# Two out-projections with operands split into high and low parts, for token tiles 2 to 4

## The chip, the cores and the metric

The kernel runs on one core of a Trainium2 chip. The time is device time in microseconds (us) of one execution. TensorE (PE) multiplies, VectorE (DVE), ScalarE (ACT) and GpSimd (POOL) work element by element, and SyncE (SP) issues most DMAs. All of them run their own instruction stream in order and wait for each other through semaphores.

## The reference

576 tokens (512 of a prompt, 64 of eight samples) of width 1024 go through two layers. Layer 0 mixes tokens by a gated delta rule and causal pooling, layer 1 by a linear recurrence with learned gates. Both end in an out-projection, and a mixture of 16 experts follows:

```python
y = jnp.concatenate([o_a, o_b], axis=-1) @ w_out          # layer 0
...
y = (hs * y_br) @ w_out                                   # layer 1
...
x = layer_norm(ALPHA * x + h, ln_mix_g[layer], ln_mix_b[layer])
f = moe(x, router_w, router_bias, moe_w_gate[layer], moe_w_up[layer], moe_w_down[layer])
x = layer_norm(ALPHA * x + f, ln_ffn_g[layer], ln_ffn_b[layer])
```

## The kernel before

Tokens lie in five tiles, four of 128 rows and one of 64. The mixer's result lies transposed in `XT` (eight blocks of 128 channels by 576 tokens). The out-projection multiplies a tile's columns of `XT` (stationary) with the eight weight blocks (`WO_A` in layer 0, `WO_B` in layer 1; 128 x 1024 each, taken in halves of 512 columns) and sums over the eight blocks in two PSUM banks. These matmuls are in plain fp32. The projections and the experts don't do that: they split each operand into a high part rounded to fp32r and a low rest, and sum three fp32r matmuls (high x high, high x low, low x high). ACT makes high parts by a copy, DVE makes low parts by a subtraction.

`out_and_route` is PE's order around it. In layer 0, `out_part` (line 967) does tiles 0 and 1, partly early, between steps of the sample states. In layer 1, line 1017 does tiles 0 and 1 block by block, as the recurrence delivers blocks (`mix_a`). In front of the last of the eight blocks stands a small transpose (line 1013) whose result DVE copies out (line 2382). Then `out_projection` (line 980) does tiles 2 and 3, the transposes of the normed tiles 0 and 1 follow (line 611), then tile 4, the transposes of tiles 2 and 3, the router's logits (line 991), the transposes and logits of tile 4. Banks alternate by tile, so that tile t waits for DVE to have read tile t-2 (`norm_sum`).

`norm` is the layer norm after the mixer (q = 0 and 2). For each tile DVE adds the bank to `X` and takes statistics (lines 2029 to 2038), ACT takes the root and scales, DVE applies gain and bias (lines 2052, 2054). After tile 4, ACT rounds and DVE splits the first expert's gate weights, and only then both copy out the last transposed tile.

The recurrence of layer 1 (`mixer1` of DVE) works in two groups of four channel blocks. A block takes a product, a few small operations, a scan over 576 tokens and a last product that writes `XT` and counts `mix_a` (line 2366). Most of these operations read two operands from SBUF. POOL multiplies gates for the first group (line 2622) and has nothing to do after that until the experts.

`experts` on SP issues the weights of the first two experts (2 MB each for gate, up and down) on one queue, and the tiles' rows (`store_rows`), each as soon as a semaphore lets it; `out_ps` counts finished out-projection tiles. POOL then gathers the rows of the first experts by an indirect DMA on a queue of its own, when the router has made the lists. PE fills that time with `keep_warm` (line 1054), 20 small matmuls whose result nobody reads, and then transposes the gathered rows (line 1060). ACT and DVE round and split the experts' weights unit by unit while PE multiplies.

`work` is one large SBUF array in which most tiles lie, at hand-written offsets; a region is given over to the next use by waits alone.

## Time and profile before

| | us |
|---|---|
| median of 3 runs | 1399.49 (1398.96 to 1399.92) |
| the profiled execution, its own time | 1398.68 |
| its span, first to last instruction | 1396.3 |
| PE busy with matmuls | 1243.7 (89%) |
| DVE busy | 972.4 (70%) |
| ACT busy | 730.6 (52%) |
| POOL busy | 172.2 (12%) |

The shares are averages over stages with different limits, and PE counts as busy as long as matmuls overlap, so they don't say what a shorter matmul stage is worth. That is read from the stage itself: who waits for whom there, and what the work costs by start-to-start time. The time of an execution is 2.4 us above its span; this rest lies around the span and is the same for any kernel's sum here.

### The profile page before, as it was taken

To read this page: it belongs to the slowest core of one execution; us is meant where nothing else is said; L and a number is where in the kernel's file an instruction comes from. 1 tells how busy PE (TensorE), PEld (TensorE's weight loads), DVE (VectorE), ACT (ScalarE), POOL (GpSimd) and SP (SyncE) were. 2 spreads that over 40 slices of the span, in tenths; PEclk is the share of its full clock that TensorE was granted. 3 is DMA by queue.
4 is the path that set the end of the run, shared out by engine and by line. 5 is a ranking of instruction groups with operands and counts; after the bars stand their busy time and mean duration, and the time that the engine had idled before them with its cause. 6 is when DMAs were issued, how large, how long until landed. Compare 5 with 4: busy or idle time off the path is not lost.

```text
span 1396.3 us, 18281 instructions
## 1 busy us (share of the span) xinstructions
PE 1243.7 (89%) x6605; PEld 1009.9 (72%) x6605; DVE 972.4 (70%) x1449; ACT 730.6 (52%) x1011; POOL 172.2 (12%) x243
## 2 busy tenths in 40 slices
PE   5999988889999699999999299989988999999970
PEld 5988887777446588888887199954456888888860
DVE  3766355441444599999997653748556999999957
ACT  2534332221012288888885652355134888888844
POOL 4101442200300010000000300010001100000002
PEclk9999999997998799999999599999988999999995
DMA  7222060001343689999994812040555899999835
GB/s 204 61 61 63 0 197 28 1 1 53 107 164 132 236 331 409 420 408 419 409 403 151 283 60 68 1 150 1 200 203 219 338 411 415 406 425 413 334 113 196
DMA packets 63101, 296.60 MB, mean 212 GB/s; under 512 B 6624, under 2 KB 32969, under 8 KB 50752
## 3 DMA queue, kind: packets, MB, share of 16 engines
q1 hardware_dynamic: 51136, 252.78, 47.0%
q0 software_dynamic: 7296, 26.22, 5.2%
q10 hardware_dynamic: 4608, 16.78, 3.0%
q8 instruction: 40, 0.66, 0.2%
q14 instruction: 21, 0.17, 0.0%
HBM read 268.87 MB, written 26.89 MB: 212 GB/s over the span
## 4 chain that ended last, share of the span: by engine, by line
PE 83%; DVE 9%; ACT 3%; issue 2%; DMA 2%; SPq 0%; POOL 0%; POOLq 0%; DVEq 0%; ACTq 0%
PE bank L1070 25%; PE bank L1097 13%; PE bank L980 6%; PE bank L624 5%; PE bank L625 4%; PE bank L650 4%; PE bank L652 4%; PE bank L967 2%; PE bank L1017 2%; PE bank L1060 2%; PE bank L1226 2%; PE bank L991 2%; PE bank L611 1%; PE bank L720 1%; PE bank L1088 1%
## 5 line engine op out<-in xcount | busy, mean ns | idle before, releaser
L1251 ACT ACTIVATE GU_HIGH<-work 128x1024 fp32r<-128x1024 f32 x256 | 270.2, 1060 | 64.9 <-PE bank L1070 60.8
L1070 PE MATMUL bank<-GU_HIGH,XGT_HIGH 128*128 128x512 f32 x512 | 203.7, 398 | 6.1 <-DVE XGT_LOW_B L2210 6.1
L2016 DVE TENSOR_TENSOR WGT_LOW<-work,GU_HIGH 128x1024 fp32r<-128x1024 f32 x128 | 155.6, 1223 | 13.5 <-ACT GU_HIGH L1251 5.5
L2016 DVE TENSOR_TENSOR WUP_LOW<-work,GU_HIGH 128x1024 fp32r<-128x1024 f32 x128 | 153.0, 1222 | 8.9 <-ACT GU_HIGH L1251 5.1
L1251 ACT ACTIVATE WDN_HIGH<-work 128x1024 fp32r<-128x1024 f32 x128 | 135.4, 1063 | 44.2 <-PE bank L1097 44.2
L2232 DVE TENSOR_TENSOR WDN_LOW<-work,WDN_HIGH 128x1024 fp32r<-128x1024 f32 x128 | 151.7, 1221 | 7.6 <-ACT WDN_HIGH L1251 3.6
L1070 PEld LDWEIGHTS bank<-GU_HIGH,XGT_HIGH 128*128 128x128 f32 x512 | 97.2, 190 | 26.1 <-DVE XGT_LOW_B L2210 6.9
L1251 ACT ACTIVATE work<-bank 128x512 f32<-128x512 f32 (+5 forms) x124 | 53.4, 469 | 113.8 <-PE bank L713 27.0
L1251 ACT ACTIVATE W_HIGH<-work 128x1024 fp32r<-128x1024 f32 x36 | 37.8, 1058 | 130.6 <-PE bank L625 80.9
L1070 PE MATMUL bank<-GU_HIGH,XGT_LOW_A 128*128 128x512 f32 x256 | 101.1, 395 | 0.0
L1070 PE MATMUL bank<-WGT_LOW,XGT_HIGH 128*128 128x512 f32 x256 | 101.0, 395 | 0.0
L1070 PE MATMUL bank<-GU_HIGH,XGT_LOW_B 128*128 128x512 f32 x256 | 100.0, 391 | 0.0
L1070 PE MATMUL bank<-WUP_LOW,XGT_HIGH 128*128 128x512 f32 x256 | 99.9, 390 | 0.0
L1097 PE MATMUL bank<-WDN_HIGH,HT_HIGH 128*128 128x512 f32 x240 | 96.4, 402 | 0.0
L1097 PE MATMUL bank<-WDN_HIGH,HT_LOW 128*128 128x512 f32 x240 | 93.7, 390 | 0.0
L1097 PE MATMUL bank<-WDN_LOW,HT_HIGH 128*128 128x512 f32 x240 | 93.5, 390 | 0.0
L980 PE MATMUL bank<-work,XT 128*128 128x512 f32 (+1 forms) x192 | 83.2, 593 | 0.0
L1466 ACT ACTIVATE lnw<-lnw 128x1 f32<-128x1 f32 (+1 forms) x10 | 2.0, 203 | 134.2 <-DVE lnw L2038 134.2
L980 PEld LDWEIGHTS bank<-work,XT 128*128 128x128 f32 (+1 forms) x192 | 32.8, 172 | 48.6 <-issue 48.0
L1760 DVE SCALAR_TENSOR_TENSOR work<-work,par 128x512 f32<-128x512 f32 x120 | 56.9, 517 | 2.1
L1934 DVE TENSOR_TENSOR W_LOW<-work,W_HIGH 128x1024 fp32r<-128x1024 f32 x20 | 25.1, 1261 | 47.2 <-ACT W_HIGH L1251 47.2
L1070 PEld LDWEIGHTS bank<-GU_HIGH,XGT_LOW_A 128*128 128x128 f32 x256 | 48.9, 191 | 10.5
(479 smaller groups left out, 2854.4 us busy)
## 6 DMA issues: line engine op xcount, KB each, us to landing
work<-in_moe_w_gate_dram SPq DMA_DIRECT2D x32, 2048.0 KB, 10.4
work<-in_moe_w_up_dram SPq DMA_DIRECT2D x32, 2048.0 KB, 10.2
work<-in_moe_w_down_dram SPq DMA_DIRECT2D x32, 2048.0 KB, 9.6
y_rows<-work ACTq DMA_DIRECT2D x32, 512.0 KB, 10.4
work<-in_ab_w_in_dram SPq DMA_DIRECT2D x10, 1024.0 KB, 5.5
work<-in_c_w_in_dram SPq DMA_DIRECT2D x8, 1024.0 KB, 5.8
x_rows<-X SPq DMA_DIRECT2D x8, 512.0 KB, 2.6
work<-in_c_w_out_dram SPq DMA_DIRECT2D x1, 4096.0 KB, 15.5
```

The source lines that it names most:

```text
L624: mm(bank[c % 2][:, 0:TH], w[:, k, :], x[:, k, 0:TH], **ends)
L625: last = mm(bank[(3, 6)[c % 2]][:, 0:TH], w[:, k, :], x[:, k, TH:T], **ends)
L650: last = mm(bank[c % 3][:, 0:TH], w[:, k, :], x[:, k, 0:TH], **ends)
L652: last = mm(bank[(3, 6, 7)[c % 3]][:, 0:TH + 2], w[:, k, :], x[:, k, TH:T + 2], **ends)
L967: last = mm(bank[2 * (t % 2) + half][0:ROWS[t], :], XT[:, k, tile_cols(t)], (WO_A, WO_B)[l][k][:, 512 * half:512 * half + 512], start=(k = ...
L980: last = mm(bank[2 * (t % 2) + half][0:ROWS[t], :], XT[:, k, tile_cols(t)], (WO_A, WO_B)[l][k][:, 512 * half:512 * half + 512], start=(k = ...
L1070: last = mm(psum, x, w, start=(k == m == 0), stop=(k == KD - 1 and m == 2))
L1097: last = mm(bank[banks[half]][:, :], x[:, f, :], w[:, f, cols], start=(f == n == 0), stop=(f == 3 and n == 2))
L1251: return nc.scalar.activation(out, in_, ACT.Copy, scale=scale)
L1760: last = V.scalar_tensor_tensor(dst, src, w, dst, ALU.mult, ALU.add)
L2016: V.tensor_tensor(low[u][:, 2 * n:2 * n + 2, :], w[u][:, 2 * n:2 * n + 2, :], high, ALU.subtract)\
L2232: V.tensor_tensor(WDN_LOW[u][:, f, :], WDN[u][:, f, :], WDN_HIGH[:, f, :].bitcast(F32), ALU.subtract).then_inc(down_split, 1)
```

## The change

Tiles 2 to 4 of both out-projections are done as three fp32r matmuls in place of one fp32 matmul. Tiles 0 and 1 stay as they were.

Layer 0: after the sample states are done and `mix_a` has counted four, ACT copies the eight weight blocks to `WO_HIGH` and, once the sample states are stored (`state_out`), tiles 2 to 4 of `XT` to `XO_HIGH`. DVE makes eight `WO_LOW` blocks and the low part of tile 2 ahead of its first norm; the low parts of tiles 3 and 4 come behind the norms of tiles 0 and 1. A low part overwrites its tile of `XT` (`XO_LOW`; the rows of the order call it XT_HIGH).

Layer 1: ACT copies `WO1_HIGH` as soon as half of the blocks are out, and `XO1_HIGH` after the last. POOL makes five of the eight `WO1_LOW` blocks, DVE the other three once the recurrence is over, then the low part of tile 2 behind the statistics of tile 0. PE takes a half's eight blocks pass by pass: first high x high, then high x low, then low x high, each with its own wait.

The new blocks lie where the first experts' weights go. So SP loads the second expert's gate weights only behind the first expert's down weights, and in layer 1 the first expert's gate weights only when the out-projection is done. Three semaphores are merged: the load of `wab_in` now counts in `hist_in`, and those of `SS` and `WG` in `delta_in`, for which each waiter waits in full.

```diff
+        WO_HIGH = [placed(f"WO_HIGH{k}", WORK_AT, off, (D,))
+                   for k, off in enumerate((12288, 13312, 14336, 15360, 16384, 19456, 20480, 21504))]
+        WO_LOW = [placed(f"WO_LOW{k}", WORK_AT, off, (D,))
+                  for k, off in enumerate((4096, 5120, 6144, 27168, 28192, 30240, 32304, 33328))]
+        XO_HIGH = {t: placed(f"XO_HIGH{t}", WORK_AT, off, (KD, ROWS[t])) for t, off in ((2, 22560), (3, 23584), (4, 34352))}
+        WO1_HIGH = [placed(f"WO1_HIGH{k}", WORK_AT, off, (D,))
+                    for k, off in enumerate((12288, 13312, 16896, 17920, 21504, 22528, 26112, 27136))]
+        WO1_LOW = [placed(f"WO1_LOW{k}", WORK_AT, off, (D,))
+                   for k, off in enumerate((8192, 9216, 10240, 11264, 30752, 14592, 15616, 19200))]
+        XO1_HIGH = {t: placed(f"XO1_HIGH{t}", WORK_AT, off, (KD, ROWS[t])) for t, off in ((2, 20224), (3, 23808), (4, 24832))}
+        XO_LOW = XT0_HIGH
+        WO_ORDER = (*range(NH, KD), *range(NH))
...
                 sp.wait_ge(mix_a, NH + KD * l)
                 sp.wait_ge(mix_b, NH)
-                for u in range(2):
-                    gate(l, u, u)
+                if l == 0:
+                    gate(l, 0, 0)
                 for t in range(NT - 1):
                     store_rows(l, 2 * l, t)
                 sp.wait_ge(out_ps, NT * (l + 1))
+                if l:
+                    gate(l, 0, 0)
                 up(l, 0, 0)
                 store_rows(l, 2 * l, NT - 1)
                 down(l, 0, 0)
+                gate(l, 1, 1)
                 up(l, 1, 1)
                 down(l, 1, 1)
...
-            sp.dma_start(wab_in, win[:, :, 2048:2056]).then_inc(wab_sem, 16)
+            sp.dma_start(wab_in, win[:, :, 2048:2056]).then_inc(hist_in, 16)
...
-            sp.dma_start(SS, state_delta[0].rearrange("s h k v -> k (s h) v")).then_inc(ss_in, 16)
-            sp.dma_start(WG, b_w_group[0].rearrange("g c d -> c g d")).then_inc(wg_in, 16)
+            sp.dma_start(SS, state_delta[0].rearrange("s h k v -> k (s h) v")).then_inc(delta_in, 16)
+            sp.dma_start(WG, b_w_group[0].rearrange("g c d -> c g d")).then_inc(delta_in, 16)
...
                 for t in tiles:
                     if t >= 2:
                         pe.wait_ge(norm_sum, 2 * l * NT + t - 1)
+                    if l == 0:
+                        pe.wait_ge(wo_split, KD + t - 1)
+                        for half in range(2):
+                            c = slice(512 * half, 512 * half + 512)
+                            for k in range(KD):
+                                high, low = XO_HIGH[t][:, k, :], XO_LOW[:, k, tile_cols(t)]
+                                for n, (x, w) in enumerate(((high, WO_HIGH), (high, WO_LOW), (low, WO_HIGH))):
+                                    last = mm(bank[2 * (t % 2) + half][0:ROWS[t], :], x, w[k][:, c],
+                                              start=(k == n == 0), stop=(k == KD - 1 and n == 2))
+                        last.then_inc(out_ps, 1)
+                        continue
+                    done = KD + NT - 2
+                    if t == 2:
+                        pe.wait_ge(wo_rounded, done + KD + 1)
                     for half in range(2):
-                        for k in range(KD):
-                            last = mm(bank[2 * (t % 2) + half][0:ROWS[t], :], XT[:, k, tile_cols(t)],
-                                      (WO_A, WO_B)[l][k][:, 512 * half:512 * half + 512], start=(k == 0), stop=(k == KD - 1))
+                        c = slice(512 * half, 512 * half + 512)
+                        for n in range(3):
+                            if t == 2 and n == 1:
+                                pe.wait_ge(wo_split_pool, 5)
+                                pe.wait_ge(wo_split, done + 3)
+                            if n == 2:
+                                pe.wait_ge(wo_split, done + 3 + t - 1)
+                            for k in range(KD):
+                                x = XO_LOW[:, k, tile_cols(t)] if n == 2 else XO1_HIGH[t][:, k, :]
+                                w = WO1_LOW if n == 1 else WO1_HIGH
+                                last = mm(bank[2 * (t % 2) + half][0:ROWS[t], :], x, w[k][:, c],
+                                          start=(k == n == 0), stop=(k == KD - 1 and n == 2))
                     last.then_inc(out_ps, 1)
...
+                if q == 0:
+                    e_dve.wait(act, 0, "s3")
+                    act.wait_ge(mix_a, NH)
+                    for n, k in enumerate(WO_ORDER):
+                        if n == NH:
+                            act.wait_ge(wo_in, 16)
+                        copy(WO_HIGH[k][:, :], WO_A[k]).then_inc(wo_rounded, 1)
+                    act.wait_ge(state_out, 16 * 8)
+                    for t in range(2, NT):
+                        copy(XO_HIGH[t][:, :, :], XT[:, :, tile_cols(t)]).then_inc(wo_rounded, 1)
+                if q == 2:
+                    act.wait_ge(wo_in, 32)
+                    act.wait_ge(mix_a, NH + KD // 2)
+                    for k in range(KD):
+                        copy(WO1_HIGH[k][:, :], WO_B[k]).then_inc(wo_rounded, 1)
+                    act.wait_ge(mix_a, NH + KD)
+                    for t in range(2, NT):
+                        copy(XO1_HIGH[t][:, :, :], XT[:, :, tile_cols(t)]).then_inc(wo_rounded, 1)
                 if q % 2 == 0:
                     for t in range(NT - 1):
...
-                dve.wait_ge(wab_sem, 16)
+                dve.wait_ge(hist_in, 16 * 6)
...
+            def split_out_x(l, t):
+
+                dve.wait_ge(wo_rounded, (KD + NT - 2) * l + KD + t - 1)
+                x = XT[:, :, tile_cols(t)]
+                V.tensor_tensor(XO_LOW[:, :, tile_cols(t)], x, (XO_HIGH, XO1_HIGH)[l][t][:, :, :].bitcast(F32), ALU.subtract)\
+                    .then_inc(wo_split, 1)
+
...
+                if q == 0:
+                    for n, k in enumerate(WO_ORDER):
+                        dve.wait_ge(wo_rounded, n + 1)
+                        V.tensor_tensor(WO_LOW[k][:, :], WO_A[k], WO_HIGH[k][:, :].bitcast(F32), ALU.subtract)\
+                            .then_inc(wo_split, 1)
+                    split_out_x(0, 2)
+                else:
+                    dve.wait_ge(mix_a, NH + KD)
+                    for k in range(5, KD):
+                        dve.wait_ge(wo_rounded, KD + NT - 2 + k + 1)
+                        V.tensor_tensor(WO1_LOW[k][:, :], WO_B[k], WO1_HIGH[k][:, :].bitcast(F32), ALU.subtract)\
+                            .then_inc(wo_split, 1)
                 dve.wait_ge(lnp_in[0], 32 * (l + 1))
                 dve.wait_ge(x_in, 64)
                 for t in range(NT - 1):
                     stats(t)
+                    if q == 2 and t == 0:
+                        split_out_x(1, 2)
                     coefficients(t)
                     finish(t)
+                    if t < 2:
+                        split_out_x(l, t + 3)
                 to_channels(q + 1, (0, 1))
...
                 half = KD // 2
                 for m in range(half):
                     gated_input(m)
+                pool.wait_ge(lru_gates_done, 2 * KD)
+                for k in range(5):
+                    pool.wait_ge(wo_rounded, KD + NT - 2 + k + 1)
+                    G.tensor_tensor(WO1_LOW[k][:, :], WO_B[k], WO1_HIGH[k][:, :].bitcast(F32), ALU.subtract)\
+                        .then_inc(wo_split_pool, 1)
```

Three places where instructions stand otherwise. POOL, at the end of the recurrent mixer, before the change (line 2622 is the gates' product, line 2579 the first gather of the experts):

```order
L2475 COPY work<-work 128x24
L2622 TENSOR_TENSOR work<-work 128x576 x4
L2579 DMA work<-x_rows,idx_all 128x1024 x2
L2582 UNCONDITIONAL_BRANCH
L2582 ISA
```

The same place now (WO_LOW_110 to 114 are `WO1_LOW` 0 to 4):

```order
L2703 TENSOR_TENSOR work<-work 128x576 x4
L2711 TENSOR_TENSOR WO_LOW_110<-work,WO_HIGH_102 128x1024
L2711 TENSOR_TENSOR WO_LOW_111<-work,WO_HIGH_103 128x1024
L2711 TENSOR_TENSOR WO_LOW_112<-work,WO_HIGH_104 128x1024
L2711 TENSOR_TENSOR WO_LOW_113<-work,WO_HIGH_105 128x1024
L2711 TENSOR_TENSOR WO_LOW_114<-work,WO_HIGH_106 128x1024
L2660 DMA work<-x_rows,idx_all 128x1024 x2
```

Five subtractions stand between the gates' products and the gather. DVE, from the recurrence's last product (line 2366, now 2447) to the first tile's norm, before:

```order
L2366 TENSOR_TENSOR XT<-work 128x576
L2380 COPY LNP<-bank 108x256
L2382 COPY LNP<-bank 72x128
L2029 SCALAR_TENSOR_TENSOR X<-X,bank 128x512 x2
L2034 BN_STATS lnw<-X 128x6 x2
L2036 BN_AGGR lnw<-lnw 128x2
L2038 TENSOR_SCALAR lnw<-lnw 128x1
```

and now:

```order
L2447 TENSOR_TENSOR XT<-work 128x576
L2461 COPY LNP<-bank 108x256
L2463 COPY LNP<-bank 72x128
L2183 TENSOR_TENSOR WO_LOW_115<-work,WO_HIGH_107 128x1024
L2183 TENSOR_TENSOR WO_LOW_116<-work,WO_HIGH_108 128x1024
L2183 TENSOR_TENSOR WO_LOW_117<-work,WO_HIGH_109 128x1024
L2094 SCALAR_TENSOR_TENSOR X<-X,bank 128x512 x2
L2099 BN_STATS lnw<-X 128x6 x2
L2101 BN_AGGR lnw<-lnw 128x2
L2103 TENSOR_SCALAR lnw<-lnw 128x1
L2081 TENSOR_TENSOR XT_HIGH<-XT,XO_HIGH_118 128x8x128
```

Three subtractions stand ahead of the first norm and one (tile 2's low part) inside it. SP, where it issues the first loads of layer 1's experts, before:

```order
L417 DMA work<-in_moe_w_gate_dram 128x4096 x2
L427 DMA x_rows<-X 128x1024 x4
L420 DMA work<-in_moe_w_up_dram 128x4096
L427 DMA x_rows<-X 64x1024
L423 DMA work<-in_moe_w_down_dram 128x4096
L420 DMA work<-in_moe_w_up_dram 128x4096
L423 DMA work<-in_moe_w_down_dram 128x4096
```

and now (the wait for `out_ps` stands ahead of the first gate load):

```order
L441 DMA x_rows<-X 128x1024 x4
L431 DMA work<-in_moe_w_gate_dram 128x4096
L434 DMA work<-in_moe_w_up_dram 128x4096
L441 DMA x_rows<-X 64x1024
L437 DMA work<-in_moe_w_down_dram 128x4096
L431 DMA work<-in_moe_w_gate_dram 128x4096
L434 DMA work<-in_moe_w_up_dram 128x4096
L437 DMA work<-in_moe_w_down_dram 128x4096
```

Both gate loads, which stood ahead of the four tiles' rows, now stand behind them; in layer 0 only the second one moves.

## Rows read from the trace of the kernel before

**Rows 1.** Chain of waits of the whole span: start us, us, engine and line.
```profile
396.76 27.47 PE bank L980 x64
...
466.05 6.57 PE bank L1054 x40
...
500.08 5.48 PE bank L1070 x24
...
956.40 24.04 PE bank L1017 x56
...
983.98 27.49 PE bank L980 x64
...
1053.44 6.43 PE bank L1054 x40
```

**Rows 2.** Timeline of DVE, layer 1: start us, us, instruction, idle before it.
```profile
971.47 0.76 DVE L2366 TENSOR_TENSOR XT<-work 128x576 f32<-128x576 f32 x1
...
978.34 0.76 DVE L2366 TENSOR_TENSOR XT<-work 128x576 f32<-128x576 f32 x1
...
982.40 1.28 DVE L2029 SCALAR_TENSOR_TENSOR X<-X,bank 128x512 f32<-128x512 f32 x2 [1.53 <-PE bank L1017]
...
985.29 0.15 DVE L2038 TENSOR_SCALAR lnw<-lnw 128x1 f32<-128x1 f32 x1
```

**Rows 3.** Timeline of DVE, layer 0, the first norm of the mixer.
```profile
390.04 1.28 DVE L2029 SCALAR_TENSOR_TENSOR X<-X,bank 128x512 f32<-128x512 f32 x2 [13.85 <-PE bank L967]
```

**Rows 4.** Timeline of SP, expert loads in layer 0 and in layer 1.
```profile
386.66 0.81 SPq L417 DMA_DIRECT2D work<-in_moe_w_gate_dram  x2
...
1027.13 0.33 SPq L420 DMA_DIRECT2D work<-in_moe_w_up_dram  x1
1034.80 0.48 SPq L427 DMA_DIRECT2D x_rows<-X  x1
```

**Rows 5.** Timeline of ACT, the end of the recurrent mixer.
```profile
964.55 2.40 ACT L1670 ACTIVATE work<-work 128x576 f32<-128x576 f32 x4
```

**Rows 6.** DVE line 1934 on its own: ns minimum/median/maximum.
```profile
L1934 DVE TENSOR_TENSOR W_LOW<-work,W_HIGH x20: 1206/1225/1973, 24.9 to 171.7; 128x1024 fp32r<-128x1024 f32 x20
```

**Rows 7.** Timeline of DVE in the first mixer.
```profile
158.23 1.97 DVE L1934 TENSOR_TENSOR W_LOW<-work,W_HIGH 128x1024 fp32r<-128x1024 f32 x1 [5.24 <-ACT W_HIGH L1251]
...
175.79 0.60 DVE L1946 TENSOR_TENSOR work<-work,inv_cnt 128x16 f32<-128x16 f32 x1
```

**Rows 8.** Timeline of POOL in the first mixer and at the first gather.
```profile
156.03 3.09 POOL L2514 TENSOR_TENSOR work<-work 128x704 f32<-128x704 f32 x2
...
175.39 1.87 POOL L2486 TENSOR_SCALAR work<-work 128x512 f32<-128x512 f32 x1
...
467.24 1.10 POOL L2579 DMA_INDIRECT work<-x_rows,idx_all  x1 [91.63 <-DVE idx_all L2202]
```

**Rows 9.** POOL by line and shape: busy us, mean ns, idle before.
```profile
L2538 POOL TENSOR_TENSOR work<-work,own_sample 64x1024 f32<-64x1024 f32 x4 | 7.5, 1888 | 36.5 <-DVE work L1876 32.4 <-PE bank L857 4.1
...
L2622 POOL TENSOR_TENSOR work<-work 128x576 f32<-128x576 f32 x4 | 5.6, 1400 | 14.0 <-ACT work L1659 14.0
```

**Rows 10.** Windows: busy PE, PEld, DVE, ACT, POOL, granted clock, DMA share, GB/s.
```profile
944.40:948.20 3.80, 3.78 (x7) 1.95 (x8) 3.62 (x11) 2.22 (x6) 0.00 (x0) 0.53 0.02 4
948.20:955.00 6.80, 6.79 (x27) 3.78 (x25) 6.54 (x16) 2.67 (x6) 0.00 (x0) 1.00 0.00 1
448.20:465.70 17.50, 7.87 (x57) 6.78 (x56) 12.77 (x49) 5.21 (x8) 0.00 (x0) 0.50 0.95 373
...
1036.00:1052.30 16.30, 6.68 (x51) 5.95 (x51) 11.87 (x45) 4.65 (x7) 0.00 (x0) 0.50 1.00 400
```

**Rows 11.** DMA issues at 467, at 1054 and from 500 to 740: us to landing.
```profile
work<-x_rows,idx_all POOLq DMA_INDIRECT x1, 4.2
...
work<-x_rows,idx_all POOLq DMA_INDIRECT x1, 4.8
...
work<-x_rows,idx_cur POOLq DMA_INDIRECT x12, 10.2
```

More of the change, by code:

```diff
@@ L290, in settle @@
                 self.engine.wait_ge(self.s, self.n)
-        x_in, hist_in, gates_in, wab_sem = sem("x_in"), sem("hist_in"), sem("gates_in"), sem("wab_in_s")
+        x_in, hist_in, gates_in = sem("x_in"), sem("hist_in"), sem("gates_in")
         w_in = [sem(f"w_in{s}") for s in range(4)]
@@ L296, in hybrid_trunk @@
         router_in, lists_zeroed = sem("router_in"), sem("lists_zeroed")
-        ss_in, wg_in, wo_in, wri_in, hist1_in = sem("ss_in"), sem("wg_in"), sem("wo_in"), sem("wri_in"), sem("hist1_in")
+        delta_in, wo_in, wri_in, hist1_in = sem("delta_in"), sem("wo_in"), sem("wri_in"), sem("hist1_in")
         wo_early_in = sem("wo_early_in")
+        wo_rounded, wo_split = sem("wo_rounded"), sem("wo_split")
+        wo_split_pool = sem("wo_split_pool")
         state_out, y_out = sem("state_out"), sem("y_out")
@@ L368, in hybrid_trunk @@
         lru_par = sem("lru_par")
-        lru_a, lru_a2, lru_t, lru_w, lru_root, lru_x, lru_h, ext1_zeroed = (
-            sem(f"lru_{n}") for n in ("a", "a2", "t", "w", "root", "x", "h", "ext_zeroed"))
+        lru_a, lru_t, lru_w, lru_root, lru_x, lru_h, ext1_zeroed = (
+            sem(f"lru_{n}") for n in ("a", "t", "w", "root", "x", "h", "ext_zeroed"))
         st1_ps, st1_out, shift_out = sem("st1_ps"), sem("st1_out"), sem("shift_out")
@@ L815, in delta_samples @@
                 e_act.wait(pe, 0, "nw")
-                pe.wait_ge(ss_in, 16)
+                pe.wait_ge(delta_in, 32)
                 e_pool.wait(pe, 0, "qd")
@@ L840, in pool_group @@
                     mm(bank[b7][:, 0:TS], WG[:, g, :], POOLED[:, g, TP:T], start=True, stop=True).then_inc(group_ps, 1)
-                pe.wait_ge(wg_in, 16)
+                pe.wait_ge(delta_in, 32)
                 pe.wait_ge(pooled_done, NH)
@@ L892, in mixer0 @@
             def mixer0():
-                pe.wait_ge(hist_in, 16 * 5)
+                pe.wait_ge(hist_in, 16 * 6)
                 for c in range(NCHUNK):
```

## The prediction

> **What bounds the kernel now.** I read the chain of waits first. There PE's own matmuls are the chain in both out-projections: line 980 stands as one unbroken piece of 27.47 us in layer 0 and of 27.49 us in layer 1 [rows 1], so what shortens those matmuls shortens the span unless something else takes their place. The piece holds 64 records for 32 products, as every fp32 product stands as two. That is 858 ns a product, and 13.74 us for a tile (16 products). In front of it in layer 1 stands line 1017, 56 records in 24.04 us, seven channel blocks of 3.434 us each.
>
> Next I asked how close DVE is behind PE. In layer 0 DVE waits 13.85 us for PE ahead of the first norm [rows 3]: it has time there. In layer 1 it has none. The recurrence ends a channel block every (978.34 - 971.47) / 2 = 3.435 us [rows 2], which is PE's pace, and the first norm begins only 3.3 us after the last of them. So layer 0 is bound by PE alone, and layer 1 by PE and DVE side by side.
>
> Last I looked at the gathers. keep_warm lies on the chain, from 466.05 to 472.62 and from 1053.44 to 1059.87 [rows 1]. The first gather is issued 1.2 us after its start (467.24) [rows 8] and lands 4.2 us later in layer 0, and 4.8 us after its issue in layer 1 [rows 11]. So the gathers are hidden with a slack of 5.4 - 4.2 = 1.2 us and 5.2 - 4.8 = 0.4 us (with the same 1.2 us between keep_warm and issue in layer 1).
>
> **PE's saving.** The experts' fp32r products run 24 in 5.48 us, 228 ns each [rows 1]; their operands have the same 512 columns. Three passes cost 685 ns in place of 858, a tile 10.96 us in place of 13.74: 2.78 us less, and 8.4 us less for tiles 2 to 4 of a layer. (Tile 4 has 64 rows, but the time goes by the 512 columns.)
>
> **Layer 0: -8.4.** The splits are extra work for ACT (eight copies and three) and DVE (eight subtractions and one before tile 2). ACT needs 2.40/4 = 0.6 us for 576 columns [rows 5], so about 1.06 for 1024 (an estimate); DVE's subtraction of 128 x 1024 has a median of 1.225 us [rows 6]. The eight pairs fit in DVE's wait of 13.85 us. What can be late is tile 2's part, for which ACT waits until the sample states are stored, the condition that lets SP issue at 386.66 [rows 4]. Copy and subtraction end at 386.66 + 1.06 + 1.22 = 389.0; DVE begins the first norm at 390.04 [rows 3] and PE tile 2 at 396.76. Without that cover the part would cost 2.3 us. Later low parts add 1.2 us to a norm of 7.4 us a tile, against PE's 10.96.
>
> **Layer 1: what POOL does to DVE.** POOL's subtractions wait for ACT's copies, which come after ACT's last step of the recurrence (966.95) [rows 5], so the first begins at 968.0, while DVE has channels 5 to 7 still to do. Do POOL and DVE disturb each other? One row says fully: DVE's subtraction that began at 158.23 took 1.97 us in place of 1.225 while POOL's TENSOR_TENSOR ran until 159.12 [rows 7, 8]; 160.20 - 1.225 = 158.98, so it began its work only 0.14 us before POOL's end. Another says briefly: the operation at 175.79, under POOL's TENSOR_SCALAR of 175.39 to 177.26, took 0.60 us and was through long before POOL's end [rows 7, 8]. POOL's operations here are TENSOR_TENSOR, as in the first, and I take full blocking, one operation each in turn.
>
> The Trainium skill bears on this (SBUF — State Buffer, section "SBUF: two separate sides"): a DVE operation with two SBUF inputs and a GpSimd operation that reads SBUF exclude each other for a whole instruction. The first row agrees, the second doesn't; by the page the change's price is that of the full blocking below, by the second row that of the rival A.
>
> A POOL subtraction of 128 x 1024 isn't in the trace. Line 2538 does 1024 elements on 64 partitions in 1.888 us, line 2622 does 576 in 1.400 [rows 9], which scaled by columns gives 2.49. I take 1.9, the row with the same columns, and keep 2.49 for the range. Five make 9.5 us; DVE gets a little back where it starts before POOL ends, so it loses some 9.2 us.
>
> Without the loss, channel 5 is out at 972.2, and PE wants it at 956.40 + 5 x 3.434 = 973.6. With it, it comes at 981.4: PE waits 7.8 us. After a wait its clock is at the lower level: 0.53 of full speed for 3.8 us in the stretch from 944.40, then 1.00 [rows 10], which loses 1.8 us. PE ends tiles 0 and 1 at 981.4 + 3 x 3.434 + 1.8 = 993.5, with the small transpose ahead of the last block 993.8, in place of 983.98: **+9.8**.
>
> **Layer 1: then DVE is late.** The copy behind that transpose ends at about 990.7; DVE's three subtractions end at 994.4, tile 0's sums and statistics (3.04 us, 982.40 to 985.44) [rows 2] at 997.4, tile 2's low part at 998.6. PE, from 993.8, does two passes of its first half (3.65 us) and wants that part at 997.5: **+1.1**. Tile 3 wants tile 1's bank read. DVE has tile 0's coefficients and gain left (4.35 us, taken from the same norm), tile 3's low part, and tile 1's sums, to 998.6 + 4.35 + 1.2 + 2.6 = 1006.8, and PE ends tile 2 at 1005.9: **+0.9**. From then on PE is ahead of nothing. Layer 1 comes to 9.8 + 1.1 + 0.9 - 8.4 = **+3.4**.
>
> **The loads that move back.** A 2 MB load takes 5.2 us at 400 GB/s [rows 10]. In layer 0 one (the second expert's gate) now stands behind tile 4's rows. The weights' bytes ended at 465.7 [rows 10], just before the gather. Now they end 5.2 us later against the program, and from the gather's first byte (1.2 us after issue, by the 1.10 us of its issue) [rows 8] they overlap it by 465.7 + 5.2 - 468.4 = 2.5 us. In layer 1 the same load moves, and the first gate load stands ahead of up: two loads, 10.4 us, in the 7.7 us between up's issue (1027.13) and tile 4's rows (1034.80) [rows 4], 2.7 us too much. The stream that ended at 1052.3 [rows 10] ends 7.9 us later, and the overlap with the gather's bytes (from 1055.8) is 4.4 us. Under an unbroken weight stream a gather lands after 10.2 us in place of 4.2 [rows 11]: behind the first 1.2 us, 9.0 in place of 3.0, so two thirds of an overlap are lost. That is 1.7 us less the slack of 1.2, **+0.5**, and 2.9 less 0.4, **+2.5**. Bounds: nothing; or the full 10.2 us in both layers (4.8 and 5.0).
>
> A rule of the Trainium skill would make this smaller (DMA: Bandwidth & Descriptors, section "Queues, rings and completion order"): each DMA engine takes turns between queues packet by packet. Half of 400 GB/s would carry the 512 KB in 2.6 us in place of 1.3, a delay of at most 1.3 us, and the two terms would be +0.1 and +0.9, the sum 2.0 us lower. The steady 10.2 us speaks against equal turns.
>
> The first gate load of layer 1 lands 12.4 us or so after tile 4's matmuls end, before the router is done: 0. The merged semaphores are waited for later than all their loads: 0.
>
> **The sum.** -8.4 + 3.4 + 0.5 + 2.5 = -2.0. The profiled execution's own time, 1398.68, lies 0.8 below the median of the runs, so 1396.7 there, and 1399.49 - 2.0 = **1397.5** as a median. That is no difference a measurement can tell (0.2%, 2.8 us). With 2.49 us a POOL operation it is 3 us more, 1400.5; with no loss at the gathers 3 us less, 1394.5. These are the own range of the likeliest case.
>
> **Rivals.** *A, POOL and DVE hardly disturb each other.* For it speaks the row of 0.60 us. If each POOL operation costs DVE nothing, +9.8 falls away, the two waits of 1.1 and 0.9 stay: -8.4 - 6.4 + 3.0 = -11.8, 1387.7. If each costs the 0.44 us of that row (0.60 less its neighbours' 0.16, an estimate), channel 7 comes 2.2 us late, of which PE had 1.4 to spare: 1388.5. If DVE keeps the port and POOL comes only after the scans, PE waits some 4 us in tile 2 for the fifth block: about 1390.7.
>
> *B, slower.* The blocking as above, and both gathers take the 10.2 us of the steady state. Then they cost 4.8 and 5.0: -8.4 + 3.4 + 9.8 = +4.8, 1404.3. The sign turns when both together cost more than 5.0 us, a mean landing of 7.8 us. Against it: the weight stream ends during the gather, where in the steady state it doesn't.
>
> *C, the saving isn't there.* Fp32r passes might not run at 228 ns with these operands, in bursts of eight with one stationary each. The experts have the same pattern, so I give this little: it lies within B's chance.
>
> **Chances.** Likeliest case 0.70, A 0.20, B and C 0.10. Of the likeliest, whose own range is 1394.5 to 1400.5, a third lies under 1396.7, nearly all the rest within 0.2%. Faster 0.20 + 0.23 = 0.43, same 0.43, slower 0.14. The range takes in A's lower end and the price of 2.49: 1387.5 to 1401.
>
> **What would show it.** Right: line 1017's successor with a PE wait of 7 to 8 us ahead of the sixth block, DVE's products and scans of channels 5 to 7 stretched by about 1.9 us each beside five POOL subtractions, short waits of PE in tile 2 and ahead of tile 3, passes of 228 ns, layer 0's piece 8.4 us shorter, and a gather in layer 1 that lands about 8 us after issue. Wrong: a recurrence at its old pace of 3.435 us (A), POOL's operations all behind the scans, or a gather that ends both times under keep_warm.

## The result, and the profile after

The changed kernel takes 1402.22 us (median of 10 runs, 1401.13 to 1407.64), the kernel before 1399.58 in the same comparison: the ratio is 1.0027, with an interval from 1.0014 to 1.0040. It is a little slower, where 1397.5 had been forecast, and 1.2 us outside the range. The profiled execution took 1401.49, its span is 1399.4, 3.1 us above that of before. (What lies around the span is not quite the same for both, 2.1 us here and 2.4 before.)

The chain of waits, before (start us, us, engine and line):

```profile
439.86 1.90 PE bank L611 x16
441.75 9.32 PE bank L991 x64
...
1059.87 0.91 PE bank L1060 x8
...
1063.26 7.36 PE bank L1070 x24
```

The same chain, after (lines 628, 1002, 1020, 1031, 1057, 1094, 1100 and 1110 are the successors of 611, 980 in layer 0, 980 in layer 1, 991, 1017, 1054, 1060 and 1070):

```profile
420.83 11.05 PE bank L1002 x48
431.88 1.75 PE bank L628 x16
433.63 10.93 PE bank L1031 x64
...
460.72 5.72 DMA work<-x_rows,idx_all
...
991.57 22.10 PE bank L1020 x96
...
1015.41 11.05 PE bank L1020 x48
```

Against [rows 1], the two out-projections are nearly as short as forecast: 48 products, one tile, take 11.05 us, 230 ns each. Layer 0's ends at 431.88, where it ended at 439.86 before: -8.0. Behind it two things are new. The router's logits (64 small products, 9.32 us before) take 10.93, and the first gather stands on the chain, where keep_warm stood. In layer 1, line 1057 breaks in two (the next view shows it) and tile 2 begins at 991.57 in place of 983.98, although the recurrence had begun 6.3 us sooner than before.

Where that goes is seen on three engines. PE's timeline, layer 1, after (idle time before an instruction and who ended it in brackets):

```profile
949.90 17.33 PE L1057 MATMUL bank<-work,XT 128*128 128x512 f32 x40
976.34 10.14 PE L1057 MATMUL bank<-work,XT 128*128 128x512 f32 x16 [9.11 <-DVE XT L2447]
...
986.42 3.60 PE L1057 MATMUL bank<-work,XT 128*128 128x512 f32 x8
991.57 2.11 PE L1020 MATMUL bank<-WO_HIGH,XO_HIGH 128*128 128x512 f32 x8 [1.54 <-DVE X L2094]
```

POOL's, the same stretch, after:

```profile
961.70 13.76 POOL L2711 TENSOR_TENSOR WO_LOW<-work,WO_HIGH 128x1024 fp32r<-128x1024 f32 x5 [35.39 <-ACT WO_HIGH L1291]
```

DVE's, from the end of one block to the end of the next, after:

```profile
961.69 0.76 DVE L2447 TENSOR_TENSOR XT<-work 128x576 f32<-128x576 f32 x1
962.36 2.92 DVE L2432 TENSOR_TENSOR work<-work 128x576 f32<-128x576 f32 x1
965.21 2.32 DVE L2433 TENSOR_TENSOR work<-XT,work 128x8 f32<-128x8 f32 x1
967.57 2.27 DVE L2436 TENSOR_TENSOR work<-work 128x8 f32<-128x8 f32 x1
...
969.90 3.42 DVE L2439 TENSOR_TENSOR_SCAN work<-XT,work 128x576 f32<-128x576 f32 x1
...
973.43 2.06 DVE L2442 COPY work<-work 128x8 f32<-128x8 f32 x1
975.52 0.76 DVE L2447 TENSOR_TENSOR XT<-work 128x576 f32<-128x576 f32 x1
```

POOL's five subtractions and DVE's steps take turns: five of DVE's next steps are each held for one of POOL's, an operation on eight columns (0.16 us elsewhere) for 2.3 us. Against the same steps elsewhere (0.75, 0.16, 0.17, 1.36 and 0.17 us) the five lose 2.17, 2.16, 2.10, 2.06 and 1.89 us. One channel block takes 975.52 - 961.69 = 13.83 us in place of 3.435. PE waits 9.11 us for it and comes back at a lower clock. Windows, after (us; busy PE, weight load, DVE, ACT, POOL with counts; granted clock, DMA share, GB/s):

```profile
967.20:976.30 9.10, 0.03 (x1) 0.00 (x0) 8.95 (x8) 0.98 (x2) 8.26 (x4) 0.77 0.00 0
976.30:981.00 4.70, 4.66 (x6) 2.08 (x7) 4.47 (x13) 0.00 (x0) 0.00 (x0) 0.50 0.01 3
981.00:986.50 5.50, 5.50 (x13) 2.26 (x13) 2.42 (x5) 2.52 (x3) 0.00 (x0) 0.87 0.08 20
986.50:990.00 3.50, 3.50 (x9) 1.26 (x8) 3.38 (x4) 0.00 (x0) 0.00 (x0) 1.00 0.04 11
```

A clock of 0.50 is the 1.2 GHz level. The piece of 16 records that takes 6.87 us at full clock (429 ns each) [rows 1] takes 10.14 here.

The clock shows in layer 0's logits as well. The 2 us in which it fell to the lower level there, before and then after (the 2 us ahead of them stand at 1.00 in both):

```profile
445.75:447.75 2.00, 2.00 (x14) 2.00 (x13) 1.75 (x2) 0.19 (x1) 0.00 (x0) 0.61 0.31 131
```

```profile
435.63:437.63 2.00, 2.00 (x15) 2.00 (x14) 1.29 (x3) 1.73 (x3) 0.00 (x0) 0.67 1.04 442
```

By these shares it fell some 4.4 us after the logits' start before, and some 2.7 us after it now.

The gather in layer 1, after, in two views: the DMA issues at 1053 (KB each, us to landing) and the chain there (PE's wait for it stands as "issue").

```profile
work<-x_rows,idx_all POOLq DMA_INDIRECT x1, 8.2
```

```profile
1052.19 7.19 PE bank L1094 x40
1059.38 2.20 issue
1061.59 1.15 PE bank L1100 x8
...
1065.21 8.50 PE bank L1110 x24
```

It landed 4.8 us after its issue before [rows 11]. Now PE runs out of keep_warm 2.2 us ahead of it, the transposes behind the wait take 1.15 us in place of 0.91, and the first products 8.50 in place of 7.36.

### The profile page after: what moved, and what is told of

It is laid out like the page before. It is cut to its first block, busy times and chain, and to the rows that moved or that the text cites. A ratio compares the mean times of both kernels' runs of the same rounds, so it can differ in the third digit from the quotient of the medians.

```text
span 1399.4 us, 18527 instructions
## 1 busy us (share of the span) xinstructions
PE 1235.0 (88%) x6701; PEld 1030.6 (74%) x6701; DVE 1001.0 (72%) x1466; ACT 750.8 (54%) x1033; POOL 185.1 (13%) x248
## 4 chain that ended last, share of the span: by engine, by line
PE 80%; DVE 11%; ACT 4%; issue 2%; DMA 2%; SPq 0%; POOL 0%; POOLq 0%; DVEq 0%; ACTq 0%
PE bank L1110 25%; PE bank L1137 13%; PE bank L641 5%; PE bank L642 4%; PE bank L667 4%; PE bank L669 4%; PE bank L1002 2%; PE bank L1020 2%; PE bank L984 2%; PE bank L1100 2%; PE bank L1266 2%; PE bank L1031 1%; PE bank L737 1%; PE bank L1128 1%; PE bank L839 1%
## 5 line engine op out<-in xcount | busy, mean ns | idle before, releaser
L1291 ACT ACTIVATE GU_HIGH<-work 128x1024 fp32r<-128x1024 f32 x256 | 270.2, 1060 | 66.4 <-PE bank L1110 62.0
L2649 POOL COPY idx_cur<-idx_all 128x1 int32 x28 | 7.0, 249 | 401.5 <-PE bank L1100 401.5
L1291 ACT ACTIVATE XGT_HIGH<-bank 128x512 fp32r<-128x512 f32 x66 | 35.3, 586 | 41.1 <-PE bank L1100 41.1
L1110 PEld LDWEIGHTS bank<-WGT_LOW,XGT_HIGH 128*128 128x128 f32 x256 | 49.1, 192 | 10.2
## 6 DMA issues: line engine op xcount, KB each, us to landing
work<-in_moe_w_up_dram SPq DMA_DIRECT2D x32, 2048.0 KB, 10.4
```

The source lines that it names most:

```text
L1110: last = mm(psum, x, w, start=(k == m == 0), stop=(k == KD - 1 and m == 2))
L1291: return nc.scalar.activation(out, in_, ACT.Copy, scale=scale)
```

## The experiments

All ratios are to the kernel before, run beside them (its medians lie between 1399.1 and 1399.6 us). The theory: the steps of DVE that POOL holds up, the clock behind waits, and the gathers behind the moved loads cost more than the passes save. Its rivals stand with each run.

**1. DVE makes all eight low blocks.**

```diff
-                    for k in range(5, KD):
+                    for k in range(KD):
                         dve.wait_ge(wo_rounded, KD + NT - 2 + k + 1)
...
-                for k in range(5):
-                    pool.wait_ge(wo_rounded, KD + NT - 2 + k + 1)
-                    G.tensor_tensor(WO1_LOW[k][:, :], WO_B[k], ...)
```

> The change, but DVE makes all eight low weight blocks of layer 1 behind the recurrence, POOL none. Theory (POOL's five subtractions take the port from DVE during the scans, which costs PE 12.4 us ahead of tile 2): the recurrence is back at 3.435 us a block, PE ends tiles 0 and 1 12.4 us sooner; DVE's subtractions take 9.3 us in place of 3.5 ahead of the first norm's sums, so PE begins tile 2 about 6.5 us sooner than with the change. 1402.2 - 6.5 = 1395.7, ratio to before 0.997. Rival (it is DVE's own extra work around the norm, or the moved loads, that cost): five more subtractions on DVE add 5.8 us, 1408, ratio 1.006.

Measured: 1397.30, ratio 1.0000 (0.9985 to 1.0015). By the medians it is 4.9 us less than the change, by the ratios 3.8, where the theory had 6.5. PE's timeline in layer 1:

```profile
949.25 24.20 PE L1055 MATMUL bank<-work,XT 128*128 128x512 f32 x56
...
984.22 3.78 PE L1018 MATMUL bank<-WO_HIGH,XO_HIGH 128*128 128x512 f32 x8 [7.22 <-DVE X L2092]
987.80 2.43 PE L1018 MATMUL bank<-WO_LOW,XO_HIGH 128*128 128x512 f32 x8
990.07 1.99 PE L1018 MATMUL bank<-WO_HIGH,XT_HIGH 128*128 128x512 f32 x8
```

The recurrence is whole again (56 records in 24.20 us), and the wait moves to the sums, 7.22 us, behind DVE's eight subtractions. From the first block to tile 2 it is 34.97 us, 6.7 less than the change's 41.67. About 2 us of that go at once: the first 16 products of tile 2 take 5.85 us (984.22 to the third pass at 990.07) in place of the change's 3.78 (the granted clock is 0.50 from 984.20 to 987.80). The rival is out.

**2. POOL writes zeros in place of subtracting.**

```diff
-                    G.tensor_tensor(WO1_LOW[k][:, :], WO_B[k], WO1_HIGH[k][:, :].bitcast(F32), ALU.subtract)\
-                        .then_inc(wo_split_pool, 1)
+                    G.memset(WO1_LOW[k][:, :].bitcast(F32), 0.0).then_inc(wo_split_pool, 1)
```

> The change, but POOL fills its five low blocks of layer 1 with zeros (it writes them and reads nothing), in the same place and with the same waits; the result lacks these low parts. Theory (DVE's two-operand steps and POOL's reads exclude each other): DVE is not stretched, channel blocks stay at 3.435 us, PE ends tiles 0 and 1 12.4 us sooner and then waits about 1.8 us for DVE's three subtractions and the sums: about 12 us less than the change, 1390, ratio 0.993. Rival (any POOL instruction on these tiles blocks DVE): DVE loses five fills of 1 us or so, about 1395.5, ratio 0.997, with products and scans stretched by about 1 us each.

Measured: 1390.12, ratio 0.9941 (0.9922 to 0.9961). Timelines of POOL, then of DVE beside it:

```profile
958.74 4.68 POOL L2711 MEMSET WO_LOW<- 128x1024 f32 x5 [35.50 <-ACT WO_HIGH L1291]
```

```profile
959.43 0.75 DVE L2432 TENSOR_TENSOR work<-work 128x576 f32<-128x576 f32 x1
960.10 0.16 DVE L2433 TENSOR_TENSOR work<-XT,work 128x8 f32<-128x8 f32 x1
...
960.53 1.36 DVE L2439 TENSOR_TENSOR_SCAN work<-XT,work 128x576 f32<-128x576 f32 x1
...
961.99 0.51 DVE L2442 COPY work<-work 128x8 f32<-128x8 f32 x1
```

POOL is busy in the same place, for 4.68 us, but it reads nothing, and DVE's two-operand steps are not stretched by a hundredth. So it is not that POOL works or writes there that holds DVE up; what the subtraction does beyond the fill is to read and subtract. The recurrence's share of the loss is some 12 us (1402.22 - 1390.12), as forecast for this run. (One copy of eight columns did wait, 0.51 in place of 0.17 us.)

**3. The gathers ahead of the second expert's up and down loads.**

```diff
                 gate(l, 1, 1)
+                sp.wait_ge(xg_in[0], arrivals(l, 1))
                 up(l, 1, 1)
```

> The change, but SP holds the second expert's up and down loads back until the first gather has landed, in both layers. Theory (the weight stream delays the gather): in layer 1 the gather lands about 5 us after its issue in place of 8.2, PE's idle 2.2 us ahead of the transposes goes, and so does most of the 1.4 us that the transposes and first products took longer at the lower clock; in layer 0 0.5 us. 1402.2 - 2.7 to 4.3, 1398 to 1399.5, ratio about 0.9995. Rival (the gather is late for the lists or the rows' stores, not for the stream): no change, 1402.2; or the second expert's weights come too late, and it is slower.

Measured: 1398.06, ratio 0.9993 (0.9977 to 1.0009), 4.2 us less than the change. The gather in layer 1, DMA issues at 1054, and the chain there:

```profile
work<-x_rows,idx_all POOLq DMA_INDIRECT x1, 4.3
```

```profile
1053.44 7.32 PE bank L1095 x40
1060.76 0.90 PE bank L1101 x8
...
1064.14 5.76 PE bank L1111 x24
```

It is hidden again, and the first 24 products take 5.76 us in place of 8.50, less even than the 7.36 of before. The weight stream, not the lists or the rows' stores, had delayed it.

**4. Layer 0's half alone.** Layer 1's products, splits and loads are those of before.

```diff
-                            for k in range(KD):
-                                x = XO_LOW[:, k, tile_cols(t)] if n == 2 else XO1_HIGH[t][:, k, :]
...
+                        for k in range(KD):
+                            last = mm(bank[2 * (t % 2) + half][0:ROWS[t], :], XT[:, k, tile_cols(t)],
+                                      WO_B[k][:, 512 * half:512 * half + 512], start=(k == 0), stop=(k == KD - 1))
...
+                gate(l, 0, 0)
+                if l:
+                    gate(l, 1, 1)
```

> Layer 0's half of the change alone; layer 1's out-projection and the order of its loads as before. Theory (the loss is all in layer 1): layer 0's two pieces of matmuls are 8.0 us shorter, of which 1.5 to 2.1 us go at the logits' clock and at the gather, so 1399.6 - 6.2 = 1393.4, ratio 0.9956. Rival (layer 0's gain is given back later, by the experts' stream or the clock): 1398 or more, ratio over 0.999.

Measured: 1394.36, ratio 0.9960 (0.9945 to 0.9975), as the theory had it: layer 0's half is worth 4.7 us and keeps them.

**5. PE kept busy in the wait for the sixth block.**

```diff
+                        if k == 5:
+                            keep_warm(40)
                         pe.wait_ge(mix_a, NH + k + 1)
```

> The change, and PE does 40 small matmuls whose result nobody reads while it waits for the sixth channel block of layer 1 (about 8.6 us of work in a wait of 9.1). Theory (3.3 of the 12.4 us that PE loses there are the lower clock behind the wait, 10.14 us for a piece that takes 6.87 at full clock): the granted clock stays at 1.0, the piece takes 6.9 us, 1402.2 - 3.3 = 1398.9, ratio 0.9995. Rival (PE is held there by DVE's pace alone, and a faster piece only waits longer at the next block): blocks 6 and 7 are out 3.4 us apart, so at most 1.5 us are gained, 1400.7 or more.

Measured: 1400.34, ratio 0.9988 (0.9974 to 1.0003). PE's timeline in layer 1:

```profile
951.70 17.33 PE L1059 MATMUL bank<-work,XT 128*128 128x512 f32 x40
968.87 9.09 PE L1096 MATMUL bank<-ident 128*128 128x128 f32 x80
978.18 7.13 PE L1059 MATMUL bank<-work,XT 128*128 128x512 f32 x16 [0.22 <-DVE XT L2449]
...
990.40 2.14 PE L1020 MATMUL bank<-WO_HIGH,XO_HIGH 128*128 128x512 f32 x8 [1.54 <-DVE X L2096]
...
1026.89 11.33 PE L1031 MATMUL bank<-rw,XT 128*128 128x16 f32 x64
```

The piece of 16 takes 7.13 us in place of 10.14, and tile 2 begins 38.70 us after the first block in place of 41.67: 3.0 us, as forecast, and not the rival's 1.5. But the logits of this execution take 11.33 us, where the change's took 8.57: 2.8 us of it are gone again before the router. That this is the edit's doing isn't shown: run 9, with the change's layer 1, takes 10.03 us there. By the medians 1.9 us are left, by the ratios 5.5; what the edit is worth, the runs' spread doesn't tell.

**6. POOL's subtractions behind the recurrence.**

```diff
-                pool.wait_ge(lru_gates_done, 2 * KD)
+                pool.wait_ge(mix_a, NH + KD)
                 for k in range(5):
```

> The change, but POOL begins its five subtractions of layer 1 only when the recurrence is over. Theory (they hurt because they run beside the scans): blocks are back at 3.435 us; POOL's subtractions then take turns with DVE's three, so that the first norm's sums end about 6.7 us after PE is done with tiles 0 and 1, and the last low block about 1.3 us after PE wants it; behind the wait PE loses about 2 us at the lower clock. Net about 4 us less than the change, 1398, ratio 0.999. Rival (the place is not what counts, POOL's time is lost wherever it runs): no gain, 1402.

Measured: 1398.33, ratio 0.9983 (0.9967 to 0.9999), as expected, and the rival is out. PE's wait for the sums, then DVE's three subtractions ahead of them:

```profile
985.27 3.78 PE L1020 MATMUL bank<-WO_HIGH,XO_HIGH 128*128 128x512 f32 x8 [6.45 <-DVE X L2094]
```

```profile
975.62 8.39 DVE L2183 TENSOR_TENSOR WO_LOW<-work,WO_HIGH 128x1024 fp32r<-128x1024 f32 x3
```

The recurrence is whole (56 records in 24.20 us), and PE waits 6.45 us for the sums in place of the 9.11 within the recurrence. The taking of turns has moved with POOL: DVE's three subtractions take 8.39 us, 3.48 in the change. The sums behind them, whose second operand lies in PSUM, take 1.27 us beside POOL's next subtraction, as elsewhere.

**7. Layer 0's half with its gather first.** Run 4, and in SP's order the line of run 3:

```diff
+                sp.wait_ge(xg_in[0], arrivals(l, 1))
                 up(l, 1, 1)
```

> Layer 0's half of the change alone, and SP holds the second expert's up and down loads until the first gather has landed, in both layers. Theory: the 0.5 us that PE waits for the gather in layer 0 and the slower transposes behind it go, 1394.4 - 0.7 = 1393.7, ratio 0.9955. Rival (the loads held back come too late for the second expert): slower than 1394.4 by some us.

Measured: 1393.69, ratio 0.9961 (0.9942 to 0.9979). It meets the expected time, but 0.7 us is less than the runs can separate from run 4.

**8. Layer 1 without POOL beside the scans.** 7, and layer 1 split with DVE alone:

```diff
+                    for k in range(KD):
+                        dve.wait_ge(wo_rounded, KD + NT - 2 + k + 1)
+                        V.tensor_tensor(WO1_LOW[k][:, :], WO_B[k], ..., ALU.subtract).then_inc(wo_split, 1)
+                        if k in (0, 1):
+                            sums(k)
+                    split_out_x(1, 2)
...
+                            if t == 2 and n == 1:
+                                pe.wait_ge(wo_split, done + k + 1)
```

> Both layers split; the gathers ahead of the second expert's up and down; in layer 1 POOL makes no low block, DVE makes the first, then the sums of tiles 0 and 1, then the other seven; PE takes each pass over both halves and waits block by block in tile 2's second pass. Theory (with the port free and the banks read early, layer 1's split is worth its 8.2 us less some 3.7 us of waits in tile 2): about 4.5 us under the layer 0 half alone with its gather, 1389, ratio 0.9925. Rival (DVE's nine subtractions take the saving back, as tile 2's second pass and tile 4's transposes wait for it): 1393 or more.

(In the code the second low block stands between the sums of tiles 0 and 1.)

Measured: 1394.77, ratio 0.9952 (0.9933 to 0.9972): the rival's side of 1393. Yet its trace has layer 1 as the theory drew it: from the first block to keep_warm 92.88 us (956.69 to 1049.57), against 97.16 in run 7 and 97.11 before. PE's timeline, and where DVE is late:

```profile
990.96 0.73 PE L1016 MATMUL bank<-WO_LOW,XO_HIGH 128*128 128x512 f32 x2 [0.41 <-DVE WO_LOW L2184]
...
1023.60 1.94 PE L628 MATMUL bank<-ident,X 128*128 128x128 f32 x16 [1.61 <-DVE X L2119]
```

The time of this execution was lost ahead of anything in which the two kernels differ: it began its first norm of layer 0 at 397.0, run 7's at 390.6 (the granted clock from 150 to 200 us was 0.87 here and 0.93 there). From there to the end it is 996.6 us against 999.8. Whether the median suffers from the same thing by chance or by the program, one trace can't tell. It stays open.

**9. Layer 1's half alone.** Layer 0's products, splits and loads are those of before.

```diff
                     if l == 0:
-                        pe.wait_ge(wo_split, KD + t - 1)
...
+                                last = mm(bank[2 * (t % 2) + half][0:ROWS[t], :], XT[:, k, tile_cols(t)],
+                                          WO_A[k][:, 512 * half:512 * half + 512], start=(k == 0), stop=(k == KD - 1))
```

> Layer 1's half of the change alone; layer 0's out-projection, splits and loads as before. Theory (the two halves add up): layer 0's half alone gave 1394.4, 5.2 us under before, so without it the change is 5 us or more above 1402.2: PE loses 12.4 ahead of tile 2 and 1.5 for the sums, saves 8.2, and loses 2 to 4 at the gather: 1407.5 to 1409.5, ratio 1.0055 to 1.007. Rival (the halves depend on each other, layer 1 loses so much only behind a changed layer 0): 1403 or less, ratio under 1.0025.

Measured: 1406.05, ratio 1.0055 (1.0036 to 1.0073): 1.5 us under the expected time, at the edge of the expected ratio. PE's timeline behind the recurrence's wait:

```profile
982.66 8.54 PE L1055 MATMUL bank<-work,XT 128*128 128x512 f32 x16 [9.11 <-DVE XT L2433]
```

The wait for the sixth block is again 9.11 us. The piece behind it takes 8.54 us, where it took 10.14 in the change: behind the same wait the lower clock cost 1.7 us here and 3.3 there. Layer 0's half gives 4.7, layer 1's takes 6.9; together that is 2.2, and the change lost 2.6. The halves add up, and the rival is out.

**10. As 8, with tile 2 of layer 1 left in fp32.**

```diff
+                    if t == 2:
+                        for half in range(2):
+                            for k in range(KD):
+                                last = mm(bank[2 * (t % 2) + half][0:ROWS[t], :], XT[:, k, tile_cols(t)],
+                                          WO_B[k][:, 512 * half:512 * half + 512], start=(k == 0), stop=(k == KD - 1))
```

> As the combined version, but tile 2 of layer 1 stays a plain fp32 product, so that DVE has a tile's time (13.7 us) for its eight subtractions and PE doesn't wait for them; tiles 3 and 4 are in three passes. Theory: layer 1 saves 2 x 2.74 = 5.5 us and no wait comes in, 5.5 us under the layer 0 half with its gather (1393.7), 1388.2, ratio 0.992. Rival (DVE's chain of norms is the bound as soon as eight subtractions stand in front of it, whichever tiles they serve): tile 4's transposes wait for it as in the combined version, 1391 or more.

Measured: 1391.72, ratio 0.9944 (0.9925 to 0.9963): 3.5 us above the theory, and on the rival's side of 1391. PE's timeline in layer 1:

```profile
951.87 24.20 PE L1057 MATMUL bank<-work,XT 128*128 128x512 f32 x56
...
979.45 13.90 PE L1010 MATMUL bank<-work,XT 128*128 128x512 f32 x32
...
1017.66 1.94 PE L628 MATMUL bank<-ident,X 128*128 128x128 f32 x16 [0.59 <-issue]
1019.43 10.59 PE L1031 MATMUL bank<-rw,XT 128*128 128x16 f32 x64
```

The stage is 5.0 us shorter than in run 7 (65.79 us in place of 70.79 from the first block to the transposes), of the 5.5 expected, and the wait at tile 4's transposes, where the rival had it, is 0.59 us in place of run 8's 1.61: DVE's subtractions are nearly hidden behind tile 2. The rest was lost elsewhere: at the logits 0.9 us go back to the clock (10.59 against 9.69), and this execution began layer 1's first block 1.6 us later than run 7's, in a stretch that the edit doesn't touch. In time it is the fastest version here that computes everything, though the runs don't separate it from run 7.

## Why the prediction was wrong

The step that failed is the price of PE's loss in the recurrence of layer 1: the working had +9.8 us, the trace shows 12.4. Beside it, the working put two effects of the clock at nothing: 1.5 us at the logits of layer 0, and 1.4 of the 4.3 us at layer 1's gather. The mechanism of the likeliest case, POOL's subtractions holding DVE up one by one, was the one that came. None of the rivals came by its own mechanism: the sign turned, as in B, but the gathers landed 5.7 and 8.2 us after issue, not 10.2. By the two traces, term by term (predicted, measured in us):

| | predicted | measured |
|---|---|---|
| layer 0's passes | -8.4 | -8.0 |
| logits of layer 0, clock | not seen | +1.5 |
| layer 0's gather | +0.5 | +0.7 |
| PE's loss in the recurrence | +9.8 | +12.4 |
| waits for DVE behind it | +2.0 | +1.5 |
| layer 1's passes | -8.4 | -8.2 |
| layer 1, tile 4 to keep_warm | 0 | -0.6 |
| layer 1's gather and the clock behind it | +2.5 | +4.3 |
| untouched stretch between the layers | 0 | -0.5 |
| sum | -2.0 | +3.1 |

**Layer 0.** The cover for the splits held: tile 2 began at 396.81 as before. The passes run at 230 to 232 ns, not 228, which is the 0.4 us that the saving lacks. Unforeseen was the stretch behind them: the clock fell to its lower level within the logits in both kernels, but sooner after the shorter out-projection. All traces agree: on PE's timeline these 64 products take 11.0 to 11.3 us in the ten kernels that split layer 0, and 9.3 to 9.5 in the two that don't (before and run 9).

**Layer 1, what POOL does to DVE.** That the operations exclude each other in full was right, and the taking of turns too: runs 1, 2 and 6 take the conflict away in three ways, and each time the recurrence is back. The size was wrong, twice. A POOL subtraction cost DVE 1.9 to 2.2 us, 2.08 in the mean, where the working came to 1.84 (9.2 / 5); the shortest of the five took POOL 2.33 us and not 1.9, between the two rows that bounded it [rows 9]. Five held the block up by 13.83 - 3.435 = 10.4 us, not 9.2. And "loses 1.8 us" for the clock was 3.3: the window it was read from [rows 10] held a shorter stretch at the lower level than the 16 records met here. In run 5, where PE is kept busy in the wait, 3.0 us of it are back on the trace. But it is no fixed price: run 9 lost 1.7 behind the same wait.

The Trainium skill's rule (SBUF — State Buffer, section "SBUF: two separate sides"), exclusion for the whole instruction between a two-operand DVE operation and a GpSimd operation that reads, agrees with the 2.27 us of an eight-column product. That a GpSimd operation that only writes leaves such operations alone agrees with run 2. The 0.60 us row [rows 7], on which rival A stood, is unexplained.

**Layer 1, DVE late.** I had put the wait at tile 2's second pass and at tile 3. It came ahead of tile 2, 1.54 us, because PE needs tile 0's bank read and DVE's three subtractions stand in front of that. The working left out this wait. At tile 3 it took 2.6 us for tile 1's sums, but the sums alone, which free the bank, take 1.28 [rows 2]; by its own numbers nothing was to be waited for there, and nothing was. That 1.5 came near the forecast 2.0 is luck.

**The loads.** The stream ran on over the gather as worked out, and "about 8 us after issue" was 8.2. Less the slack of 0.4 the delay is 8.2 - 4.8 - 0.4 = 3.0 us, where the term had 2.5. (keep_warm ran 0.8 us longer as well, 7.19 in place of 6.43, but inside that delay: a faster one would have waited longer.) The rest of the 4.3 is the clock, which the term left out: the transposes and the first products behind the wait ran 1.4 us longer (0.91 to 1.15 and 7.36 to 8.50). This share isn't fixed either: in run 9 PE waited 2.80 us at the same place and lost 0.6 behind it (1.25 and 7.58). Run 3 got back 4.2 us of the 5.0 of both layers. The estimate of 1.3 us at most, from the rule of turns packet by packet (the Trainium skill, DMA: Bandwidth & Descriptors, section "Queues, rings and completion order"), was too low for layer 1: the trace shows 8.2 - 4.8 = 3.4.

## What to carry to other kernels

POOL, when it reads from SBUF beside DVE's scans and two-operand products, is no free hand: its time is taken from DVE nearly in full (10.4 us for five subtractions here), so give it work where DVE reads from PSUM, as in run 6's sums, or waits. Price a new wait of TensorE with the clock behind it, as a range and not as a figure: here 1.7 to 3.3 us on top of the same wait of 9.1, and 0.6 to 1.4 on top of waits of 2.8 and 2.2. And where loads are moved back, look at who fetches something small behind them, and hold the loads that nobody needs yet.

## What was not expected of the hardware

DVE's one-operand copy of eight columns was held up as well, 2.06 us beside a POOL subtraction and 0.51 beside a fill, where it takes 0.17 alone. The copy of one column just ahead of it was not (0.15 us).

The same 64 small logit products take from 8.49 to 11.33 us from kernel to kernel, by where in them the clock falls from its upper to its lower level. In layer 0 the shorter out-projection ahead of them moved that point forward in every kernel that has it, and 1.5 of the 8.0 us gained there were lost in the logits. In layer 1 no such pattern shows: with the same layer 1 the products took 8.57 us in the change and 10.03 in run 9.

Stretches that no edit touches differ by several us between executions: the first norm of layer 0 begins between 387.1 and 397.0 in the profiles here. Edits worth 1 or 2 us can't be told apart by the medians, and had to be read from stage to stage.
